# Applying an RMSNorm's token factor behind the matmul in a two-layer streaming encoder on one core

## The reference, cut to what matters

```python
def _rmsnorm(x, g):
    y = x * lax.rsqrt(jnp.mean(x * x, axis=-1, keepdims=True) + NORM_EPS)
    return y * g
def _swiglu(x, w_in, w_out):
    gate, up = jnp.split(x @ w_in, 2, axis=-1)
    return (jax.nn.silu(gate) * up) @ w_out
...
for li in range(2):
    hn = _rmsnorm(h, w['norm_mix_g'][li])
    h = h + mixer(hn)            # layer 0: RG-LRU and attention, layer 1: mLSTM
    h = h + _swiglu(_rmsnorm(h, w['norm_ffn_g'][li]), w['ffn_w_in'][li], w['ffn_w_out'][li])
    h = h + jax.nn.sigmoid(h @ w['ple_w_gate'][li]) * (p[li] @ w['ple_w_proj'][li])
y_out = _rmsnorm(h, w['final_g'])
```

## Time and profile before

| | before |
|---|---|
| median of 3 runs | 2903.98 us |
| the profiled execution | 2904.33 us |
| its span, first to last instruction | 2902.5 us |
| mean granted TensorE clock | 0.977 |
| busy: PE, PEld, DVE, ACT, POOL | 2753.8, 2686.8, 1274.1, 598.8, 939.6 us |
| instructions | 40640, of which 17273 matmuls |
| DMA | 160.09 MB, 55 GB/s |

### The profile page before, as it was taken

How to read it: one execution, slowest core, us unless ns; L and a number is a source line. 1 busy time by engine, 2 the same in 40 slices (tenths; PEclk the granted TensorE clock), 3 DMA queues, 4 the chain that set the end, 5 groups by cost and what they waited for, 6 DMA issues and landing times.

```text
span 2902.5 us, 40640 instructions
## 1 busy us (share of the span) xinstructions
PE 2753.8 (95%) x17273; PEld 2686.8 (93%) x17273; DVE 1274.1 (44%) x2070; ACT 598.8 (21%) x1315; POOL 939.6 (32%) x439
## 2 busy tenths in 40 slices
PE   7999998999999999996999998799999999999996
PEld 5898898999999999996999987598999999999996
DVE  7844474333333333557733037537333333333465
ACT  4515322000000000223122145412100000000042
POOL 3222043333334433332434310023433333333430
PEclk9999899999999999998999999999999999999998
DMA  3110121111111111112122221311111111111111
GB/s 135 32 30 30 47 72 38 51 44 44 44 44 44 51 51 45 44 44 105 45 68 84 85 85 54 128 54 44 44 51 44 44 45 51 44 44 44 52 37 60
DMA packets 59765, 160.09 MB, mean 55 GB/s; under 512 B 9276, under 2 KB 30268, under 8 KB 58304
## 3 DMA queue, kind: packets, MB, share of 16 engines
q1 hardware_dynamic: 29952, 109.07, 12.4%
q10 hardware_dynamic: 29632, 48.42, 4.7%
HBM read 137.07 MB, written 20.40 MB: 54 GB/s over the span
## 4 chain that ended last, share of the span: by engine, by line
PE 87%; DVE 7%; ACT 3%; issue 1%; DMA 0%; ACTq 0%; POOL 0%; DVEq 0%; POOLq 0%
PE ps L385 27%; PE ps L387 27%; PE ps L386 27%; DVE tmp L906 1%; PE ps L775 1%; DVE rstd L857 1%; PE ps L587 1%; PE ps L557 1%; PE ps L812 1%; DVE xl L914 1%; DVE hb L1344 1%; PE ps L569 0%; DVE cs L1318 0%; DVE ybuf L901 0%; PE ps L814 0%
## 5 line engine op out<-in xcount | busy, mean ns | idle before, releaser
L385 PE MATMUL ps<-xh,wh 128*128 128x352 f32 x3432 | 1125.3, 328 | 18.0 <-issue 10.3
L386 PE MATMUL ps<-xl,wh 128*128 128x352 f32 x3432 | 1116.3, 325 | 0.0
L387 PE MATMUL ps<-xh,wl 128*128 128x352 f32 x3432 | 1116.0, 325 | 0.0
L427 POOL TENSOR_TENSOR wh<-raw,seeds 128x1024 fp32r<-128x1024 f32 x208 | 419.5, 2017 | 1877.4 <-PE ps L387 1871.9
L385 PEld LDWEIGHTS ps<-xh,wh 128*128 128x128 f32 x3432 | 653.3, 190 | 25.4 <-issue 13.6
L386 PEld LDWEIGHTS ps<-xl,wh 128*128 128x128 f32 x3432 | 653.2, 190 | 2.3 <-issue 1.0
L387 PEld LDWEIGHTS ps<-xh,wl 128*128 128x128 f32 x3432 | 652.8, 190 | 0.0
L429 POOL TENSOR_TENSOR wl<-raw,wh 128x1024 fp32r<-128x1024 f32 x208 | 522.0, 2509 | 16.3
L990 DVE TENSOR_TENSOR tmpb<-ps,tmpa 128x352 f32<-128x352 f32 x132 | 69.0, 524 | 858.5 <-ACT tmpa L1483 857.4
L385 PE MATMUL ps<-hh,wh 128*128 128x352 f32 x1056 | 340.4, 322 | 0.0
L387 PE MATMUL ps<-hh,wl 128*128 128x352 f32 x1056 | 340.0, 322 | 0.0
(11 more groups left out here) (252 smaller groups left out, 2354.8 us busy)
## 6 DMA issues: line engine op xcount, KB each, us to landing
raw<-wstream SPq DMA_DIRECT2D x208, 512.0 KB, 3.6
vod<-stage ACTq DMA_DIRECT2D x72, 128.0 KB, 1.9
vb<-vod ACTq DMA_DIRECT2D x9, 512.0 KB, 3.9
ob<-vod ACTq DMA_DIRECT2D x9, 512.0 KB, 3.7
x<-xT ACTq DMA_DIRECT2D x3, 1408.0 KB, 8.5
x<-xT ACTq DMA_DIRECT2D x2, 2112.0 KB, 7.6
xsave<-x ACTq DMA_DIRECT2D x1, 4224.0 KB, 11.4
x<-xsave ACTq DMA_DIRECT2D x1, 4224.0 KB, 14.7
```

The costliest lines, as they stand in the source:

```text
L385: pe.matmul(out, whi, mhi, start=first, stop=False)
L386: pe.matmul(out, whi, mlo, start=False, stop=False)
L387: return pe.matmul(out, wlo, mhi, start=False, stop=last)
L427: pool.tensor_tensor(hi, raw[:, r, :], zero, ALU.add).then_inc(hi_made, 1)
```

## The change

**What it does.** The token factor is the same for all features of a token, so it can be multiplied onto the columns behind the matmul. Norms 0 to 3 now make `xh` as a ScalarE copy of x scaled by g, and `xl` in one VectorE instruction from x, g and `xh`; `tmp` goes. The factor `rstd` is kept for all 1056 tokens and applied where results leave PSUM:

- First projection: VectorE copies every unit out with a multiply by `rstd` (`in0_out`), Gelu is a ScalarE step in place (`gelu`), and the q copies in attention go to VectorE (`fill_out`). The order of units is `IN0`: blocks 0 to 3 token tile by token tile, then blocks 4 to 9 block by block, then the last four for tile 0. The sum over the eight squares of an input token is done by VectorE (`input_sum`), with one `norm_sum` per tile on PE. The LRU's gates stand behind units 11, 14, 17 and 23.
- FFN: VectorE scales the gate and the up bank (`scale`), ScalarE's silu works in SBUF, the product reads SBUF.
- Layer 1's mixer: the gate rows are scaled through `gtmp`, `uu` is scaled on VectorE ahead of each convolution, v and o by ScalarE's `scale` with one factor per partition (`rcol`, made by nine small transposes), the kept conv rows through `ctail`.
- Tail phases: two highs and two lows of tile 0 behind each of u = 16 or 17 to 20, of tile 1 behind the next four; `norm_sum` behind u = 18 and 22 for norms 1 to 3.
- Loads: x's three tiles are issued together, five constant loads move from ScalarE's queue to SP's, behind the fourth weight block; `dist` is loaded after the first norm.

**The diff, cut to its core.**

```diff
+        IN0 = ([(p, tt) for tt in range(NT) for p in range(4)] + [(p, tt) for p in range(4, 10) for tt in range(NT)]
+               + [(p, 0) for p in range(10, 14)])
...
@@ sync
+                if p == 3:
+                    sp.dma_start(ua[:, :, 3 + TP:6 + TP], I["a_conv"]).then_inc(m0_in, 16)
+                    sp.dma_start(lbd[:, :, :, :], I["lbd"]).then_inc(m0_in, 16)
...
@@ tensor
-                    if u == 17 or u == 21:
-                        norm_sum(ni, (u - 17) // 4)
+                    first = 18 if ni < 4 else 17
+                    if u == first or u == first + 4:
+                        norm_sum(ni, (u - first) // 4)
...
-                                pe.wait_ge(h32_ready, pair - 2)
+                                pe.wait_ge(pair_read, pair - 2)
...
-                            pe.wait_ge(h32_ready, pairs + u // 2 + 1)
+                            pe.wait_ge(pair_read, pairs + u // 2 + 1)
...
-            input_sums()
-            for p in range(10):
-                dense((B0_IN + p) % NW, B0_IN + p, FREE0["in0"] - 6 + 3 * p, (OFF["in0"] + 3 * p) % 6,
-                      XLN["mix0"] if p == 0 else None)
...
+            for u, (p, tt) in enumerate(IN0):
+                pe.wait_ge(acc_free, FREE0["in0"] - 6 + u + 1)
...
+                if u in (2, 6, 9):
+                    norm_sum(0, (2, 6, 9).index(u))
+                if u == 11:
                     pe.wait_ge(m0_in, 16 * 5)
...
+                if u in (11, 14, 17):
+                    lru_gates((11, 14, 17).index(u))
...
@@ vector
+            def low(ni, tt, k):
...
+                dve.wait_ge(xh_ready, XLN[stage] + KT * tt + k + 1)
+                dve.scalar_tensor_tensor(xl[:, k, sl], x[:, k, sl], vec(gname, k), xh[:, k, sl].bitcast(F32),
+                                         ALU.mult, ALU.subtract).then_inc(xl_ready, 1)
...
             def tail_phase(ni, add):
...
                     add(u)
                     if u >= 1:
                         add_squares(ni, u - 1)
-                    if u == 17 or u == 21:
-                        scaled_part(ni, (u - 17) // 4, 0, 4)
-                    if u == 18 or u == 22:
-                        scaled_part(ni, (u - 18) // 4, 4, KT)
+                    if ni < 4 and u >= 17:
+                        for k in (0, 1):
+                            low(ni, (u - 17) // 4, 2 * ((u - 17) % 4) + k)
+                        if u == 20:
+                            rstd_of(ni, 0)
...
                 add_squares(ni, 23)
-                scaled_part(ni, NT - 1, 0, KT)
+                if ni < 4:
+                    for k in (6, 7):
+                        low(ni, 1, k)
+                    for k in range(KT):
+                        low(ni, 2, k)
+                    rstd_of(ni, 1)
+                    rstd_of(ni, 2)
...
             def ffn(layer):
...
+                    def scale(v):
...
+                        dve.tensor_tensor(tmpa[:, v % 3, :], bank(2 * tt), rstd[:, sl], ALU.mult).then_inc(gate_scaled, 1)
+                        dve.tensor_tensor(tmpb[:, v % 3, :], bank(2 * tt + 1), rstd[:, sl],
+                                          ALU.mult).then_inc(pair_read, 1)
+                    def product(v):
+                        dve.wait_ge(pair_read, 6 * cx + v + 1)
+                        dve.wait_ge(sil_ready, 6 * cx + v + 1)
+                        dve.tensor_tensor(tmpb[:, v % 3, :], tmpb[:, v % 3, :], tmpa[:, v % 3, :],
+                                          ALU.mult).then_inc(h32_ready, 1)
...
                     for v in range(6):
-                        dve.wait_ge(sil_ready, 6 * cx + v + 1)
-                        if 6 * cx + v >= 2:
-                            dve.wait_ge(hl_ready, 6 * cx + v - 1)
-                        dve.tensor_tensor(tmpb[:, v % 2, :], bank(2 * (v % 3) + 1), tmpa[:, v % 2, :],
-                                          ALU.mult).then_inc(h32_ready, 1)
-                        if v >= 1:
-                            low(v - 1)
+                        if 6 * cx + v >= 3:
+                            dve.wait_ge(hl_ready, 6 * cx + v - 2)
+                        scale(v)
+                        if v >= 1:
+                            product(v - 1)
+                        if v >= 2:
+                            low(v - 2)
+                    product(5)
+                    low(4)
                     low(5)
...
+            for k in range(KT):
+                low(0, 0, k)
+            input_sum(0)
+            for k in range(KT):
+                low(0, 1, k)
+            rstd_of(0, 0)
+            outs(0, 1)
+            input_sum(1)
+            outs(2, 3)
...
+            rstd_of(0, 2)
...
+            outs(8)
...
             conv(0)
+            outs(9, 10, 11)
...
+                    step.mark(dve.tensor_tensor(uu[:, n, 3:3 + TP], uu[:, n, 3:3 + TP], rstd[:, 0:TP], ALU.mult))
...
@@ scalar
             def high(ni, tt, k):
-                act.wait_ge(xt_ready, 1 + KT * (3 * ni + tt) + k + 1)
-                act.activation(xh[:, k, tt * TW:(tt + 1) * TW], tmp[:, k % 4, :], ACT.Copy).then_inc(xh_ready, 1)
...
+                act.activation(xh[:, k, sl], x[:, k, sl], ACT.Copy, scale=vec(gname, k)).then_inc(xh_ready, 1)
...
-                        act.activation(tmpa[:, v % 2, :], bank(2 * tt), ACT.Silu).then_inc(sil_ready, 1)
+                        act.wait_ge(gate_scaled, 6 * cx + v + 1)
+                        act.activation(tmpa[:, v % 3, :], tmpa[:, v % 3, :], ACT.Silu).then_inc(sil_ready, 1)
...
-            act.dma_start(O["c_conv_o"][:, :, 0:3], uu[:, :, TP:TP + 3]).then_inc(cconv_sent, 16)
-            act.dma_start(O["c_conv_o"][:, :, 3:6], uu[:, :, 3 + TOK:6 + TOK]).then_inc(cconv_sent, 16)
             row_exps()
```

More of the change, by code:

```diff
@@ L440, in _ @@
         def _(pe):
[L441 to L450, removed]
-            def norm_sum(ni, tt):
-                pe.wait_ge(sq_added, sums_at(ni, 12 + 4 * tt + 3))
+            def norm_sum(ni, tt):
+                if ni == 0:
+                    pe.wait_ge(in_added, added_at(tt))
+                    src = sqsum_i
+                else:
+                    pe.wait_ge(sq_added, sums_at(ni, 12 + 4 * tt + 3))
+                    src = tail_sums(ni)[0]
                 pe.wait_ge(rt_ready, 1 + 3 * ni + tt // 2)
-                pe.matmul(bank(6 + tt % 2), ones[:, :], tail_sums(ni)[0][:, tt * TW:(tt + 1) * TW],
+                pe.matmul(bank(6 + tt % 2), ones[:, :], src[:, tt * TW:(tt + 1) * TW],
                           start=True, stop=True).then_inc(ss_done, 1)
@@ L935, in tail_phase @@
                 for u in range(skip, 24):
+                    if ni == 4 and u == 23:
+                        rstd_of(4, 1)
+                        for k in range(3):
+                            final(1, k)
                     add(u)
@@ L1068, in _, with input_sum @@
             dve.tensor_scalar(sp8, mx, -8.0, None, ALU.mult).then_inc(sp_ready, 1)
-            norm(0)
+            def input_sum(tt):
+                sl = slice(tt * TW, (tt + 1) * TW)
+                for j in range(KT - 1):
+                    n = KT * tt + j + 1
+                    dve.wait_ge(sq_ready, n + 1)
+                    if j:
+                        dve.wait_ge(in_added, (KT - 1) * tt + j)
+                    a = sqx[:, (KT * tt) % 12, :] if j == 0 else sqsum_i[:, sl]
+                    dve.tensor_tensor(sqsum_i[:, sl], a, sqx[:, n % 12, :], ALU.add).then_inc(in_added, 1)
@@ new lines, in outs @@
+            def outs(*units):
+                for u in units:
+                    in0_out(u)
+            for k in range(KT):
+                low(0, 0, k)
+            input_sum(0)
+            for k in range(KT):
+                low(0, 1, k)
[3 more added lines that the diff above has]
+            outs(2, 3)
+            for k in range(KT):
+                low(0, 2, k)
+            rstd_of(0, 1)
+            input_sum(2)
+            outs(4, 5, 6, 7)
+            rstd_of(0, 2)
@@ L1622, in _ @@
             act.dma_start(O["v_o"], vt[:, TOK - P - TS:TOK]).then_inc(kv_sent, 16)
+            for j in range(3):
+                values(j)
             gates(3)
@@ L1625, in _ @@
             root_of_a(3)
-            copy_out(6)
-            for j in range(3):
-                values(j)
-            copy_out(7)
-            copy_out(8)
-            copy_out(9)
+            for t in range(AT):
+                gelu(t)
             act.wait_ge(h_ready, AT)
```

398 lines of the change are left out of this document (217 added, 181 removed).

## The result

The changed kernel takes 2953.36 us (median of 4 runs, 2951.0 to 2954.63), the kernel before, in the same comparison, 2904.42 (4 runs, 2901.82 to 2908.62). The ratio is 1.0166, 95% interval [1.0149, 1.0184]: slower by 49 us.

A forecast was written before the change was run, and what follows sets the result against it. TensorE, busy 95% of the span, bounds the kernel; only its waits matter. 64 + 24 - 19 - 7 - 6 - 5 = +51 on the profiled 2904.33 gives 2955 us; own range 2935 to 2970, with rivals 2 to 4 2908 to 2976.

The forecast's parts named there:

- FFN, +64 and +24: Ninth down unit: TensorE waits 3.2 us in 20 chunks for VectorE held by splits, +64; slower clock behind, +24.
- Into layer 1's mixer, -19: Crossing into layer 1's mixer: 12.5 us lost instead of 31.7, with a 9.8 wait for the last sum.
- Into layer 0's FFN, -7: Crossing into layer 0's FFN: 10.4 us lost instead of 17.4, 7.9 of it waiting behind held operations.
- Into layer 1's FFN, -6: Crossing into layer 1's FFN: 2 + 1 us lost instead of 9.2.
- The start, -5: First projection: earlier first unit, less slow matmuls, norm matmuls and a 7.5 us wait at the first gates; net -5.
- At nothing: covered, but nearly full: First stage: 34 output copies moved to VectorE cost some 20 us there, hidden by TensorE's PSUM banks ahead; 0.
- Rival 3: First stage: VectorE becomes the bound through copies behind the LRU scans; start +15 instead of -5, 2975; chance 0.10.
- No stall in the FFN: Ninth down unit: the five operations take 6 us or less, so no stall; 2867; chance 0.12.
- A clock that stays at 2.4 GHz: FFN: the stalls come, but TensorE's clock does not fall behind them; 2931; chance 0.20.
- Smaller crossings: Crossings between stages: gain only 10 us instead of 32, as splits run in one block; 2977; chance 0.06.
- The mean of the subtraction: FFN, profile after: the subtraction's mean near 1.8 us, the new product's as long, as a sign of the hold.

The follow-up runs named there:

- e1_pool_ffn: First experiment: changed kernel, with GpSimd's splits of the two blocks freed at the sixth up-pair held until the first add, in 20 FFN chunks; 2870.59 us.
- e2_psum: Second experiment: changed kernel, with the scaled up half written back to its PSUM bank and the product reading it there; 2874.99 us.
- the doses: Three runs of the changed kernel with four, three or two held VectorE operations left ahead of the FFN's first add, instead of five; with two, ratio 0.9869.
- e6_cross: e1_pool_ffn plus GpSimd's last freed blocks at the three crossings held until the next stage's 24 low parts are made; 2845.34 us.
- e9_double: e1_pool_ffn plus VectorE's PSUM copies for units 12 to 23 of the input projection done twice; one run, 2866.4 us.
- e7_all: e6_cross plus GpSimd held at the start, three of four blocks split only after the first convolution; 2844.9 us.

## Why the prediction was right

**FFN, +64 and +24: right, and shown.** 20 stalls of 3.03 (predicted 20 x 3.2); from matmul start to matmul start each costs 3.19, 63.8 in all. The mechanism step by step: the first four operations ended with the splits, the fifth was free, the first add came 10.0 us behind the first split (predicted 961.3 to 971.4: 10.1). The first experiment takes the stall away by POOL's timing alone, the second by PSUM alone, and the doses show the steps of one split each.
The Trainium skill, "SBUF — State Buffer", section "SBUF: two separate sides", says that the engine that starts first keeps the shared ports for its whole instruction; the trace agrees (four operations, four splits) and adds that while VectorE has such operations queued, one gets in between two consecutive splits. The changed kernel has 279 pairs of splits less than 0.2 us apart; in 109 of them no two-input operation ended between the two ends, in 169 one, and in a single one two, the second of them a small one of 0.17 us.
The clock: 13 of 20 stalls are followed by a granted clock of 0.50, which is 1.2 GHz (the window from 541.4 has 14 matmuls, the one from 689.8 at 1.00 has 21). The two layers lost 43.9 + 42.5 - 63.8 = 22.6 beside the stalls, where 24 was predicted for the clock. By the starts of the matmuls each fall cost 1.6 (13 steps of 0.29 in place of 0.16), as predicted, 21 in all; there were 13 falls where I had counted on 15, and 1.6 us are not accounted for.

**Into layer 1's mixer, -19: right.** Wait for the sum 9.8, predicted 9.8; the window from 1309 to 1400 lost 31.7 and now loses 12.4 (91 - 488 x 0.161), predicted 12.5. The stretch gained 2.6 more than those 19.3, 1.3 of it at the transposes of the gate rows, where PE's wait fell from 6.0 to 4.7; I had that at nothing. **Into layer 0's FFN, -7:** measured -8.7, the wait 8.3 where I had 7.9. **Into layer 1's FFN, -6:** measured -3.7, so this small term was too large. The wait was 2.5 where I had 2.0, and the sum left out the clock behind it: in the 3.3 us from 2005.8 on, right behind this wait, the granted clock was 0.50 and PE began 13 matmuls. e6_cross, which takes away nearly all of the three waits by POOL's timing, shows that they were VectorE's held queue.

**The start, -5: right in sum (-4.8), wrong in one part, and the close match is partly luck.** First projection matmul 18.35 (near 20), wait at the first gates 4.9 (7.5), clock low behind it (0.50 from 77.3 to 87.4). That is 2.6 less than I had, and PE waits 2.7 at the transposes of v, where it waited 0.7 before and where I had nothing: the two nearly cancel. "At nothing: covered, but nearly full" for VectorE's copies doesn't hold for more of them: e9_double shows some 2.3 us for twelve more. What the 34 moved copies cost by themselves was not measured. The slack I counted on, six PSUM banks ahead, is real for the copies: none of PE's waits up to 215 us is for one of them, but for the 0.6 for `qt` in attention, which the kernel before had too. The waits are for the convolutions and for ScalarE's part of the recurrences, which come late by what stands ahead of them on VectorE. Rival 3 (VectorE bound in the first stage) was thus right about the place and wrong about the size: it gave +15 where the trace shows -4.8.

**The other rivals.** No stall in the FFN (2867): falsified by the trace, and its condition, 1.2 us an operation, by the doses; e1_pool_ffn shows what it would have been, 2870.6. That is also the value of the rest of the change: -33.6 against my -37. A clock that stays at 2.4 GHz (2931): it fell 13 times. Smaller crossings (2977): they gave 34 where I had 32.

**One detail was off.** The mean of the subtraction was 1.61 us where I had 1.8, and the product's 1.18 where I had 1.8 too: those that meet no split take 0.52 and pull the mean down, as in the earlier trace rows.

Not tried: what the missing norm ahead of the first projection is worth by itself, the order by token tile by itself, and the kernel before with GpSimd held back.

## What to carry over

An operation's price depends on where its inputs lie: beside one of GpSimd's weight splits, a VectorE operation with two SBUF inputs costs the rest of that split, and a queue of n of them costs n splits, as long as so many follow each other (four held operations 9.6 us, three 7.0, two 4.8); with one input in PSUM it took its 0.5 us. So before moving a factor behind a matmul, list what stands ahead of the first result that TensorE wants, count the SBUF-SBUF operations beside splits, and either delay the splits until they are through (here GpSimd had 14 us of slack: 24 down units of 0.97 less its four splits) or put the wanted result first. A mean over all instances hides this: the product's 1.2 us was 0.5 where it met no split and up to 2.2 where it did. And where a wait is taken away in a stretch with a second, near-full engine, look for the next wait before counting the gain.

## What was not expected of the hardware

- The clock does not fall behind every stall of one size. Stalls of 3.03 us were followed by the low level 13 times of 20, stalls of 2.6 eight times of 20, in the same place of the same loop.
- The hold goes both ways. GpSimd's high split takes 1.90 and its low split 2.40 beside free or PSUM operations (e1_pool_ffn, 537.12 and the next), but 2.17 and 2.56 beside held 352-wide operations; beside the recurrence's 1059-wide ones in e7_all it took 2.91 and 2.75.
- The first convolution step, `uc<-ua,vecs`, has one large SBUF input and is held as well: 0.83 alone, 2.40 beside a split. The reciprocal has one SBUF input too and isn't: 2.35 us beside two splits (67.31 in the changed kernel), and 2.35 on average without any.
- An operation that reads and writes its PSUM bank in place takes 0.52, like one that writes SBUF, and is not held (533.96 in e2_psum, beside the split from 533.55).
